# Split operands in place of full fp32 products in one attention branch of a two-layer hybrid block

## The reference, cut to what matters

```python
q = rmsnorm(to_heads(q, 4, 128), q_norm_w)
k = rmsnorm(to_heads(k, 2, 128), k_norm_w)
if rope:
    q, k = rope_2d(q, rows, cols), rope_2d(k, rows, cols)
# latent queries read context and latent keys; context queries read context keys
s = einsum('bhgqd,bhkd->bhgqk', q, k) * 128 ** -0.5
p = softmax(s, axis=-1)
o = einsum('bhgqk,bhkd->bhgqd', p, v)
```

## Time and profile before

| What | Value |
|---|---|
| median of three runs | 2999.7 us (2998.19 to 2999.82) |
| the profiled execution: time, span | 3000.03 us, 2998.2 us |
| TensorE busy, share of the span | 2828.2 us, 94% |
| VectorE, ScalarE, GpSimd busy | 1502.5, 1233.9, 165.9 us |
| mean granted TensorE clock | 0.991 |
| DMA | 273.59 MB, mean 91 GB/s |
| D attention, layer 0 and layer 1 (first scores to last residue) | 104.53 and 75.65 us |

### The profile page before, as it was taken

The page is one execution under the profiler, slowest core; times in us unless marked ns, Lnnn a source line. Parts: engine busy times, 40 slices in busy tenths (PEclk is TensorE's granted clock), DMA queues, the critical chain, the costliest instruction groups (busy, mean ns, idle before and its releaser), DMA issues. The chain is left out here.

```text
span 2998.2 us, 38375 instructions
## 1 busy us (share of the span) xinstructions
PE 2828.2 (94%) x15368; PEld 2308.8 (77%) x15368; DVE 1502.5 (50%) x2348; ACT 1233.9 (41%) x2155; POOL 165.9 (6%) x188
## 2 busy tenths in 40 slices
PE   6999999999999999999999999999998899999998
PEld 4887786778778778888888878777566676788887
DVE  4258753446553445664344443873446544554444
ACT  4434434434553443544233344443445544442222
POOL 0022210000000000000000000230000000000000
PEclk8999999999999999999999999999999999999999
DMA  5122231032222223243333232224031130423332
GB/s 207 57 101 96 92 138 54 22 105 76 75 84 78 67 95 120 92 141 113 112 112 112 78 107 71 84 85 138 11 96 50 43 102 22 151 85 98 93 97 91
DMA packets 84817, 273.59 MB, mean 91 GB/s; under 512 B 9520, under 2 KB 9776, under 8 KB 83888
## 3 DMA queue, kind: packets, MB, share of 16 engines
q1 hardware_dynamic: 74896, 229.84, 23.6%
q0 software_dynamic: 9760, 41.50, 4.3%
HBM read 245.07 MB, written 26.22 MB: 90 GB/s over the span
## 5 line engine op out<-in xcount | busy, mean ns | idle before, releaser
L717 PE MATMUL slot<-Hh,wh 128*128 128x512 f32 (+1 forms) x2384 | 869.9, 366 | 30.6 <-DVE wl L1849 9.2
L717 PE MATMUL slot<-Hh,wl 128*128 128x512 f32 (+1 forms) x2384 | 836.1, 352 | 0.0
L717 PE MATMUL slot<-Hl,wh 128*128 128x512 f32 (+1 forms) x2384 | 835.5, 351 | 0.0
L717 PEld LDWEIGHTS slot<-Hh,wh 128*128 128x128 f32 x2384 | 452.7, 190 | 99.0 <-issue 25.8
L1849 DVE TENSOR_TENSOR wl<-raw,wh 128x1024 fp32r<-128x1024 f32 (+1 forms) x332 | 379.6, 1144 | 289.2 <-ACT wh L1328 286.5
L1328 ACT ACTIVATE wh<-raw 128x1024 fp32r<-128x1024 f32 (+1 forms) x332 | 323.2, 974 | 435.8 <-PE slot L717 356.5
L717 PEld LDWEIGHTS slot<-Hh,wl 128*128 128x128 f32 x2384 | 452.0, 190 | 61.5
L717 PEld LDWEIGHTS slot<-Hl,wh 128*128 128x128 f32 x2384 | 453.2, 190 | 58.6 <-issue 6.0
L717 PE MATMUL slot<-Uh,wh 128*128 128x512 f32 (+1 forms) x776 | 273.9, 353 | 0.0
L717 PE MATMUL slot<-Ul,wh 128*128 128x512 f32 (+1 forms) x776 | 273.4, 352 | 0.0
L717 PE MATMUL slot<-Uh,wl 128*128 128x512 f32 (+1 forms) x776 | 273.0, 352 | 0.0
(11 more groups left out here) (258 smaller groups left out, 3847.1 us busy)
## 6 DMA issues: line engine op xcount, KB each, us to landing
raw<-w_dram SPq DMA_DIRECT2D x204, 512.0 KB, 3.5
raw<-w_gate_dram SPq DMA_DIRECT2D x64, 512.0 KB, 3.6
ada_g_raw<-ada_dram POOLq DMA_DIRECT2D x48, 512.0 KB, 3.8
ada_g_raw<-ada_dram SPq DMA_DIRECT2D x32, 512.0 KB, 3.8
raw<-w_merge_dram SPq DMA_DIRECT2D x64, 256.0 KB, 2.8
g_kept<-logits_out SPq DMA_DIRECT2D x32, 384.0 KB, 2.3
SS<-g_kept SPq DMA_DIRECT2D x32, 384.0 KB, 3.6
ada_first<-ada_dram SPq DMA_DIRECT2D x8, 1024.0 KB, 17.8
```

The source lines that it names most:

```text
L717: return pe.matmul(dst, lhsT, rhs, start=start, stop=stop)
```

## The change

Queries, keys, values and turned probabilities of D are each split into a rounded part and a rest, as the weights are. Scores become Yh·KD_HIGH + Yl·KD_HIGH + Yh·KD_LOW, values VD_HIGH·PT + VD_LOW·PT + VD_HIGH·PT_LOW. ScalarE rounds q and k (a new copy for each of the six, placed in a later job of the projection, the last after it), rounds v in place of its plain copy, and writes `PT` as fp32r by the same copy as before. VectorE makes the rests: six of q and k, two of v (from PSUM), and one for each turned unit (from PSUM, at the head of its step). The unit banks and the value products now wait for VectorE's rest (`pt_low`) instead of ScalarE's copy, and slots 1 and 3 come free with `v_low`.

```diff
+        PT["D"] = at("PT_D", [NB, SEQ], f32r, (R_S + 7) * ROW)
+        PT_LOW = [at(f"PT_low{k}", [NB // 2, SEQ], f32r, first * ROW) for k, first in enumerate((R_S, R_X + 6))]
+        KD_HIGH, KD_LOW = rows("KD_high", R_X + 2, D_KV, f32r), rows("KD_low", R_X + 4, D_KV, f32r)
...
@@ TensorE, project @@
-                        transposes(beside, slot[beside], VT[branch][j % 2], NB, copied).then_inc(tr_done.sem, 1)
+                        transposes(beside, slot[beside], VT[branch][j % 2], NB, v_low if branch == "D" else copied).then_inc(tr_done.sem, 1)
@@ TensorE, attention @@
+                turned = pt_low if branch == "D" else pt_ready
...
+                            if branch == "D" and tile["first"] and len(tile["keys"]) == NB and h % (D_HEADS // D_KV) == 0:
+                                pe.wait_ge(d_low.sem, w.next(d_low, 1 if h else D_SPLITS - 1))
...
-                                    last = mm(out_s[:, lo:hi], QY[:, h, qs_], KD[:, h // (D_HEADS // D_KV), lo:hi])
+                                    mm(out_s[:, lo:hi], Yh[:, h, qs_], KD_HIGH[:, kv, lo:hi], start=True, stop=False)
+                                    mm(out_s[:, lo:hi], Yl[:, h, qs_], KD_HIGH[:, kv, lo:hi], start=False, stop=False)
+                                    last = mm(out_s[:, lo:hi], Yh[:, h, qs_], KD_LOW[:, kv, lo:hi], start=False, stop=True)
...
-                        pe.wait_ge(pt_ready.sem, w.next(pt_ready, values_in))
+                        pe.wait_ge(turned.sem, w.next(turned, values_in))
...
-                                last = mm(values_at[:, 0:tile["width"]], V[:, tile["h"] // 2, m * P:(m + 1) * P], pt, **flags)
+                                mm(dst, VD_HIGH[:, kv, block], pt, start=x == 0, stop=False)
+                                mm(dst, VD_LOW[kv][:, block], pt, start=False, stop=False)
+                                last = mm(dst, VD_HIGH[:, kv, block], low, start=False, stop=flags["stop"])
...
-                            pe.wait_ge(*slots.next(("unit", units % 2), pt_ready))
+                            pe.wait_ge(*slots.next(("unit", units % 2), turned))
@@ ScalarE, project: split_into_high in a job's begin, three jobs later @@
+                    if branch == "D":
+                        dst = Yh[:, j, 0:nq] if kind == "q" else KD_HIGH[:, j, :]
+                        act.activation(dst, src[:, 0:nq] if kind == "q" else src, ACT.Copy).then_inc(d_high.sem, 1)
+                        return
...
+                            act.activation(VD_HIGH[:, j, :], slot[beside][:, 0:T], ACT.Copy).then_inc(v_high.sem, 1)
...
+                    split_into_high(*plan[D_SPLITS - 1])
@@ VectorE, project @@
+                        if branch == "D" and n > 2:
+                            between = lambda: low_of_d(nq, *plan[n - 3])
...
+                    if branch == "D" and n > 0 and plan[n - 1][0] == "v":
+                        j = plan[n - 1][1]
+                        dve.wait_ge(v_high.sem, w.next(v_high))
+                        dve.tensor_tensor(VD_LOW[j], slot[1 + 2 * ((n - 1) % 2)][:, 0:T], VD_HIGH[:, j, :].bitcast(f32),
+                                          ALU.subtract).then_inc(v_low.sem, 1)
+                if branch == "D":
+                    low_of_d(nq, *plan[D_SPLITS - 1])
+
+            def low_of_d(nq, kind, j):
+
+                dve.wait_ge(d_high.sem, w.next(d_high))
+                if kind == "q":
+                    ins = dve.tensor_tensor(Yl[:, j, 0:nq], QY[:, j, 0:nq], Yh[:, j, 0:nq].bitcast(f32), ALU.subtract)
+                else:
+                    ins = dve.tensor_tensor(KD_LOW[:, j, :], KD[:, j, :], KD_HIGH[:, j, :].bitcast(f32), ALU.subtract)
+                ins.then_inc(d_low.sem, 1)
@@ VectorE, attention, at the head of step i @@
+                    if branch == "D" and LAG < i <= len(tiles) + LAG:
+                        tile = tiles[i - LAG - 1]
+                        for lo, hi in key_units(tile):
+                            span = slice(tile["col"], tile["col"] + P)
+                            dve.wait_ge(pt_high.sem, w.next(pt_high))
+                            dve.tensor_tensor(PT_LOW[lo // 3][:, 0:hi - lo, span],
+                                              unit_bank(units)[:, 0:(hi - lo) * P].rearrange("p (b s) -> p b s", s=P),
+                                              PT["D"][:, lo:hi, span].bitcast(f32), ALU.subtract).then_inc(pt_low.sem, 1)
+                            units += 1
```

More of the change, by code:

```diff
@@ L353, in col @@
             return cols[:, layer, COL[name] + k:COL[name] + k + 1]
-        COPIES = {b: sum({"r": 0, "v": 2}.get(kind, 1) for kind, _ in PROJ[b]) for b in BRANCHES}
+        COPIES = {b: sum({"r": 0, "v": 1 if b == "D" else 2}.get(kind, 1) for kind, _ in PROJ[b]) for b in BRANCHES}
+        D_SPLITS = sum(kind != "v" for kind, _ in PROJ["D"])
         B_SPLITS = sum(kind != "v" for kind, _ in PROJ["B"])
@@ L438, in build @@
         PT = {"A": at("PT_A", [NB, SEQ], f32, (R_S + 4) * ROW), "B": at("PT_B", [NB, SEQ], f32, (R_S + 7) * ROW)}
-        PT["D"] = PT["B"]
+        PT["D"] = at("PT_D", [NB, SEQ], f32r, (R_S + 7) * ROW)
+        PT_LOW = [at(f"PT_low{k}", [NB // 2, SEQ], f32r, first * ROW) for k, first in enumerate((R_S, R_X + 6))]
+        KD_HIGH, KD_LOW = rows("KD_high", R_X + 2, D_KV, f32r), rows("KD_low", R_X + 4, D_KV, f32r)
+        VD_HIGH = rows("VD_high", R_X, D_KV, f32r)
+        VD_LOW = [rows(f"VD_low{k}", row, 1, f32r)[:, 0, :] for k, row in enumerate((R_S + 11, R_S + 2))]
         QS = rows("QS", R_X, B_HEADS, f32r)
@@ L1196, in attention @@
                         tile = tiles[i - LAG - 1]
-                        pe.wait_ge(pt_ready.sem, w.next(pt_ready, values_in))
+                        pe.wait_ge(turned.sem, w.next(turned, values_in))
+                        if branch == "D" and i - LAG - 1 == LB - 1:
+                            pe.wait_ge(v_low.sem, w.next(v_low, D_KV))
                         values_in = 0
@@ L1515, in split_into_high @@
                     act.wait_ge(roped.sem, w.next(roped))
-                    src = rotated("B", kind, j)
+                    src = rotated(branch, kind, j)
+                    if branch == "D":
+                        dst = Yh[:, j, 0:nq] if kind == "q" else KD_HIGH[:, j, :]
+                        act.activation(dst, src[:, 0:nq] if kind == "q" else src, ACT.Copy).then_inc(d_high.sem, 1)
+                        return
                     for g in range(B_KV):
@@ L1536, in project @@
                             act.preload_act_table_set(EXP_AND_LN)
-                        split_before = branch == "B" and n > 0
-                        p = begin_job(between=(lambda: split_into_high(*plan[n - 1])) if split_before else None)
+                        split_before = branch == "B" and n > 0 or branch == "D" and n > 2
+                        p = begin_job(between=(lambda: split_into_high(*plan[n - (3 if branch == "D" else 1)])) if split_before else None)
                         copy_out(n, plan[n][0], plan[n][1], slot[2 * p])
@@ L1668, in branch_a @@
                     if h == 0:
-                        act.wait_ge(roped.sem, w.next(roped, 2 + (6 if layer else 0)))
+                        act.wait_ge(roped.sem, w.next(roped, 2))
                         act.activation(KR_HIGH, KR, ACT.Copy).then_inc(a_high.sem, 1)
@@ L2076, in project @@
                     if n < len(plan):
-                        split_before = branch == "B" and n > 0
-                        p = begin_job(between=(lambda: rope_and_split(nq, n - 1)) if split_before else None)
+                        between = None
+                        if branch == "B" and n > 0:
+                            between = lambda: rope_and_split(nq, n - 1)
+                        if branch == "D" and n > 2:
+                            between = lambda: low_of_d(nq, *plan[n - 3])
+                        p = begin_job(between=between)
                         kind, j = plan[n]
```

13 lines of the change are left out of this document (11 added, 2 removed).

## The result

| | before | after |
|---|---|---|
| median of 12 runs each | 2999.7 us (2995.2 to 3002.5) | 3012.1 us (3004.1 to 3017.5) |
| profiled execution | 3000.0 us, span 2998.2 | 3016.6 us, span 3014.9 |
| mean granted clock, profiled execution | 0.991 | 0.987 |
| attention of branch D, layer 0 and 1 | 104.5 and 75.7 us | 109.6 and 82.7 us |

The ratio of the runs is 1.0040, interval 1.0029 to 1.0050: slower by 0.4%, clear of the 0.2% that can be told from no change. One of the 27 later runs of the kernel before, at a mean clock of 0.40, took 7120 us and is left out of every ratio.

The account below looks back on a forecast made before the run. TensorE, busy 2828 of 2998 us, was taken as the bound, with the hand-over ring deciding in D's attention. Attention +2.8 (19.0 idle less 16.2 work) and start +2.3 gave +5.1 on 3000.0: 3005.1 us, range 2998 to 3013.

Parts of the forecast that it names:

- its own case: Whole kernel: the forecast of 3005.1 us as reckoned, 3002 to 3009, given a chance of 0.60.
- the side of slower: Whole kernel: outcomes told as slower than before, chance 0.44, against 0.50 for same and 0.06 for faster.
- a longer subtraction and a longer start: Upper end of the range, 3013 us: VectorE's subtraction at its upper bound (3011) plus a longer wait before first scores.
- Products: TensorE, branch D's attention: split products 0.23 us apart at 512 columns and 0.12 at 256.
- A rest of 384 columns at 0.55 us: VectorE, each turned unit: one subtraction out of PSUM takes 0.55 us and holds the queue for 0.475, 72 times.
- The ring of 3.5 us: Wide tile in D's attention: maximum, exponential, copy, two subtractions, next maximum take 3.5 us, against TensorE's 2.8 and 3.1.
- The rival of a longer ring: D's attention: each subtraction costs over 0.50 us of queue through separate waits or blocks; 3007 to 3009.5 us, chance 0.18.
- The start: Start of D's attention: TensorE waits for the rest of v1, first scores 1.15 us later, twice: +2.3 us.
- What hides: Projection: ScalarE's six roundings and VectorE's six rests of q and k lie in existing waits and cost nothing.
- the stepped order: D's attention: three engine queues stepped through instruction by instruction with trace durations; +2.8 us, layer 0 +0.6, layer 1 +2.2.
- the saved 16.2 us of products: TensorE, D's attention: scores save 7.4 us wide and 0.6 narrow, values 7.7 and 0.6, 16.2 less work in sum.
- the added 19.0 us of idle time: TensorE, both attentions: waits for VectorE's subtractions raise idle time from 10.6 to 29.6 us, 19.0 more.

Follow-up runs that it names:

- in_waits: Changed kernel plus 52 products with overwritten results where TensorE waits, before each attention's first scores and wide value groups, some waits moved ahead: 3003.9 us, ratio 1.0008.
- scores_only: Changed kernel with only q and k split, v and turned probabilities left fp32 as in the kernel before: 2997.2 us, ratio 0.9996.
- filler: Changed kernel plus four products of 256 columns with overwritten results before each wide tile's scores in branch D: 3020.6 us, ratio 1.0082.

## Why the prediction was right or wrong

The forecast was 3005.1 us, within 3002 to 3009 for its own case and 2998 to 3013 in all; 3012.1 lies in the range, over the case, and on the side of slower that had 0.44. That the range holds it is partly luck: its upper end was made of a longer subtraction and a longer start, and what filled it was the clock, which is in no term. The steps:

- **Products**: right, 0.23 and 0.12 us apart at full speed. The 216 ns that the Trainium skill gives for an isolated product (TensorE: Matmul & The Clock Gate, section on the back-to-back issue gap) are 0.01 under what stands in this trace. With 0.216 and 0.11 over the forecast's own counts the work saved would have been 5.5 us more, not about 4.
- **A rest of 384 columns at 0.55 us**: right, 552 ns over 64 of them, 1.02 for two. **The ring of 3.5 us**: right, 3.52. The rival of a longer ring gave 3007 to 3009.5 and came nearer to the time, but that is luck: its mechanism, more than 0.50 us of queue for each rest, did not happen: the next maximum starts 0.94 us after the two rests, 0.47 for each.
- **The start**: right in its mechanism and mis-sized. First scores came 1.44 us later relative to the projection (idle 2.54 and 2.57 for 1.10), 2.9 in sum for 2.3. The stepped 0.05 us from the end of v1's rest to the first scores was too little; the trace has 0.39 (2490.11 to 2490.50).
- **What hides**: right. The rests of q and k and the roundings show in no wait of TensorE: it has the same waits as before in layer 0's projection but for the start, and the stretch between the attentions is 1.5 us shorter than before.
- **Value groups in layer 1** came 25.6, 43.7, 62.9 and 75.3 us after the first scores, where the stepped order had 23.6, 42.0, 59.6 and 71.9. The distances were 18.2, 19.2 and 12.5 for 18.4, 17.6 and 12.4: the first comes late by the slow start, the third by the slow stretch at 2533 to 2539.
- **The step that failed** is the one that took the saved 16.2 us of products and the added 19.0 us of idle time as two separate terms, with "the clock at full speed" of the earlier trace rows carried over to the new order. Measured, TensorE's busy time fell by 3.3 and its idle time rose by 15.3 us, to 25.2 where 29.6 was forecast (22.9 of it waits for rests, and 5.1 more at the two starts, for about 29 in sum). The idle term was 3.7 us too large, and 12.9 us are missing from the saving: products that ran at 1.2 GHz. By the clock column they come to (1 - 0.95) x 109.6 + (1 - 0.92) x 82.7 = 12 us, an estimate that takes none of this time to turn into waiting were the products faster, and without them the two attentions would have been near 104.1 and 76.0 us, against 104.4 and 77.6 stepped at full clock (105.1 and 77.8 forecast). in_waits gives the same answer from the other side: at a clock of 1.00, layer 0 took 105.1, with 5.5 us of added products in its waits.

The twelve timed runs of the change agree. Those whose mean clock was 0.990 or 0.991 took 3004.1, 3006.2 and 3006.8 us, those at 0.985 and 0.986 took 3017.5, 3017.0 and 3017.5. The forecast is near the time of the first three, though this does not make it right: the kernel before varies in the same way (2993.0 us at 0.995, 3008.7 at 0.989), and like must be compared with like. That the clock differs between runs of one kernel, and that the time follows, is seen in these runs; it was not changed by itself.

Still open: which wait costs how much (in_waits filled two kinds at once), and why the clock fell behind some waits and not behind others of the same length. Behind the waits of layer 1's second and fourth value groups (1.98 and 1.23 us) it was 0.66 and 0.57 over 4 us in the first profiled run of the change, and 1.00 behind the same waits (1.96 and 1.24) in the second.

## What to carry to other kernels

Before an expensive operation is traded for cheap ones plus a helper on another engine, write down the ring of hand-overs that the helper joins and ask for the place in it where the engine already waits; here the same instructions, one place earlier in two queues, took 20 us less. A wait added to TensorE should be priced together with the speed of the products behind it: read the clock column of the short windows behind the longest waits, not only of the whole stretch. And an engine that is busy for half of the span can pass on most of what is added to it (26 to 32 of 34 us here).

## What the runs showed of the hardware that was not expected

In a kernel whose TensorE is busy for 94% of the span, waits of 1.2 to 2.6 us were followed, not every time, by stretches of a few us at 1.2 GHz, in which the products of 512 columns stood 0.43 us apart instead of 0.23. Both value groups of layer 0 that waited 2.4 us for their rests had one behind them. The first of them, and the clock in the window after it, in the profiled run of the change:

```profile
1025.53 0.50 PE L724 MATMUL slot<-PT_D,VD_high 128*128 128x512 f32 x1 [2.38 <-DVE PT_low L2353]
```

```profile
1025.50:1029.50 4.00, 3.97 (x12) 3.22 (x13) 1.69 (x4) 0.99 (x2) 0.00 (x0) 0.67 0.25 68
```

The clock is 0.67 there, and 0.65 behind the other. The kernel before, with waits of 1.1 us and less in the same stretches, had none in its profiled run. A short wait is no guarantee, though: scores_only had one at the start of layer 1, behind 1.20 us,

```profile
2480.79 0.77 PE L724 MATMUL slot<-KD_high,Yh 128*128 128x512 f32 x1 [1.20 <-ACT V L1572]
```

```profile
2480.79:2484.79 4.00, 4.00 (x13) 3.35 (x14) 3.12 (x4) 1.65 (x3) 0.00 (x0) 0.61 0.00 1
```

and none at the start of layer 0, behind the same 1.20. The fall did not always follow at once: at layer 1's start the first products came at full speed in one profiled run (0.30 us apart) and at half in the other (0.56). The Trainium skill (TensorE: Matmul & The Clock Gate, section on a second HAM failure mode, PSUM-queue depth-cycling) describes this for another kernel: short idle times of TensorE between groups of products, as it goes around the PSUM banks, let its clock alternate between the two levels, and throughput suffers though most products run at full speed. The traces here agree in this: most products stood 0.23 apart, and by the estimate above 12 us were lost. Here it was single waits for another engine, not the going around of the banks by itself.

Products without a use, put into such waits, made the kernel faster: 52 of them, 6.4 us. Put where TensorE was not waiting (filler), they cost more than the clock gave back.
